# A two-block transformer kernel on one core: convolution taps spread anew, GpSimd taken out of the gates, and the end of each residual projection rearranged

## What is computed

```python
def first_block(x, mem, ...):
    mem_n = rmsnorm(mem, norm_mem_w)
    h = x
    h = h + head_group_mixer(rmsnorm(h, norm_mix_w), ...)     # conv_module and retention, then @ w_out
    h = h + memory_cross_attention(rmsnorm(h, norm_xattn_w), mem_n, xq_w, xkv_w, xo_w)
    h = h + sq_relu_mlp(rmsnorm(h, norm_mlp_w), mlp_up_w, mlp_down_w)
    return rmsnorm(h, norm_f_w)

def conv_module(a, b, conv_w, conv_b, ln_w, ln_b):
    u = a * sigmoid(b)
    y = depthwise causal convolution of u, 31 taps, 512 channels
    return silu(layer norm of y)

def second_block(x, mem, ...):
    x = x + hybrid_mixer(rms_norm(x, norm_mix_g), ...)        # ends in merged @ w_out
    x = x + memory_cross_attention_2(rms_norm(x, norm_xa_g), mem, ...)
    x = x + swiglu(rms_norm(x, norm_ffn_g), w_gate, w_up, w_down)
    return rms_norm(x, final_g)
```

## Time and profile before

| | |
|---|---|
| three runs | 981.06, 982.01, 983.94 us; median 982.01 |
| profiled execution | 980.71 us, of which the span of the program's instructions is 979.0 |
| PE busy | 930.6 us of the span (95%) |
| DVE, ACT, POOL busy | 651.3, 475.1, 12.6 us |
| granted TensorE clock, mean | 0.987 |

### The profile page before, as it was taken

The page is one execution under the profiler, slowest core; times in us unless marked ns, Lnnn a source line. Parts: engine busy times, 40 slices in busy tenths (PEclk is TensorE's granted clock), DMA queues, the critical chain, the costliest instruction groups (busy, mean ns, idle before and its releaser), DMA issues.

```text
span 979.0 us, 15122 instructions
## 1 busy us (share of the span) xinstructions
PE 930.6 (95%) x6344; PEld 858.0 (88%) x6344; DVE 651.3 (67%) x933; ACT 475.1 (49%) x533; POOL 12.6 (1%) x40
## 2 busy tenths in 40 slices
PE   6899999599989999999999999999899899999996
PEld 6788998479879999999899999999798799999995
DVE  5799879959665555555865886765776555555555
ACT  6666435256454444444545636653474453343342
POOL 1100000000000000000000000000000000000000
PEclk9989999799999999999999999999999999999998
DMA  9646535325335565565555535545443346556551
GB/s 323 227 154 229 169 130 175 126 93 168 127 129 173 181 201 175 185 200 173 178 189 172 173 130 172 167 152 194 150 155 115 129 148 204 179 177 199 182 172 43
DMA packets 112469, 164.47 MB, mean 168 GB/s; under 512 B 2784, under 2 KB 90464, under 8 KB 112416
## 3 DMA queue, kind: packets, MB, share of 16 engines
q1 hardware_dynamic: 111856, 161.87, 49.9%
q0 software_dynamic: 560, 1.84, 0.5%
HBM read 162.64 MB, written 1.05 MB: 167 GB/s over the span
## 4 chain that ended last, share of the span: by engine, by line
PE 83%; DVE 8%; ACT 3%; DMA 3%; issue 2%; SPq 0%; DVEq 0%; ACTq 0%
PE ps L534 27%; PE ps L535 26%; PE ps L536 26%; DVE w_lo L1431 2%; DMA w_ring<-in_w_in 2%; ACT w_hi L1017 1%; DVE xl L1457 1%; ACT xh L1047 1%; PE ps L625 1%; DMA w_ring<-in_w_q_xa 1%; PE ps L661 0%; PE ps L796 0%; DVE h L1487 0%; DVE acc L1960 0%; DVE mem_l L1446 0%
## 5 line engine op out<-in xcount | busy, mean ns | idle before, releaser
L1431 DVE TENSOR_TENSOR w_lo<-w_ring,w_hi 128x2048 fp32r<-128x2048 f32 x147 | 335.7, 2291 | 151.8 <-ACT w_hi L1017 150.4
L534 PE MATMUL ps<-xh,w_hi 128*128 128x256 f32 x1216 | 347.3, 286 | 10.2 <-DVE w_lo L1526 8.9
L535 PE MATMUL ps<-xl,w_hi 128*128 128x256 f32 x1216 | 345.1, 284 | 0.0
L536 PE MATMUL ps<-xh,w_lo 128*128 128x256 f32 x1216 | 345.0, 284 | 0.0
L1017 ACT ACTIVATE w_hi<-w_ring 128x2048 fp32r<-128x2048 f32 x147 | 279.6, 1909 | 101.6 <-DMA w_ring<-in_w_in 28.5
L534 PEld LDWEIGHTS ps<-xh,w_hi 128*128 128x128 f32 x1216 | 234.1, 193 | 13.3 <-DVE w_lo L1526 8.9
L535 PEld LDWEIGHTS ps<-xl,w_hi 128*128 128x128 f32 x1216 | 234.3, 193 | 0.7
L536 PEld LDWEIGHTS ps<-xh,w_lo 128*128 128x128 f32 x1216 | 234.3, 193 | 0.0
L534 PE MATMUL ps<-w_hi,xh 128*128 128x512 f32 x192 | 77.7, 405 | 7.7 <-DVE w_lo L1431 5.1
L534 PE MATMUL ps<-w_hi,ff_h 128*128 128x512 f32 x216 | 84.3, 390 | 0.0
L535 PE MATMUL ps<-w_lo,ff_h 128*128 128x512 f32 x216 | 84.2, 390 | 0.0
(11 more groups left out here) (289 smaller groups left out, 1129.4 us busy)
## 6 DMA issues: line engine op xcount, KB each, us to landing
w_ring<-in_w_in SPq DMA_DIRECT2D x36, 1024.0 KB, 5.1
w_ring<-in_mlp_up_w SPq DMA_DIRECT2D x16, 1024.0 KB, 5.5
w_ring<-in_mlp_down_w SPq DMA_DIRECT2D x16, 1024.0 KB, 4.8
w_ring<-in_w_gate_ffn SPq DMA_DIRECT2D x11, 1024.0 KB, 5.3
w_ring<-in_w_up_ffn SPq DMA_DIRECT2D x11, 1024.0 KB, 5.3
w_ring<-in_w_down_ffn SPq DMA_DIRECT2D x11, 1024.0 KB, 5.0
w_ring<-in_xkv_w SPq DMA_DIRECT2D x8, 1024.0 KB, 5.7
w_ring<-in_w_out SPq DMA_DIRECT2D x8, 1024.0 KB, 4.9
```

The lines of the kernel that those rows point to most:

```text
L534: pe.matmul(o, lh, rh, start=first, stop=False)
L535: pe.matmul(o, lh, rl, start=False, stop=False)
L536: return pe.matmul(o, ll, rh, start=False, stop=last)
L1431: dve.tensor_tensor(w_lo[:, s, :], w_ring[:, s, :], w_hi[:, s, :].bitcast(F32), ALU.subtract).then_inc(lo_done, 1)
```

## The change

1. **Gates.** `scale_sigmoid` on GpSimd is gone. DVE multiplies `a` with the scales into `u_pad` and later `u_pad` with the sigmoid; `sig1` has two buffers, both gates' first halves come early.
2. **Memory transposes** stand between slabs 6 and 7 on PE. ACT splits slab 8 before the memory, DVE too.
3. **Taps** are spread anew over the same places; the last ones now stand behind `lo(26)`.
4. **Around the convolution's norm** PE does the variance before the tb 1 half of slab 27, and slab 28 in one piece.
5. **Boundaries.** The last slab is done for tb 1 by column halves (`form_b_last`), the first of which signals `half_done`; DVE's `lo(nxt + 1)` stands behind the splits, not ahead of the residual's addition.
6. **Attention output.** The last `hi` and `lo` of the output projection stand ahead of the split of the last head.
7. **The end.** Column halves there too; addition and gain alternate; GpSimd has no part; the square root takes six operations, not nine, and one operation ahead of it is gone.

```diff
+            def form_b_last(i, k0, xt, kks, half, last, step=0):
+                pe.wait_ge(lo_done, weight_count(i) + step)
+                wh, wl = slab(i, D)
+                c = slice(half * HALF, (half + 1) * HALF)
+                for kk in kks:
+                    mm = mm3(tok(2 + half), (xt[0][:, k0 + kk, P:S], xt[1][:, k0 + kk, P:S]), (wh[:, kk, c], wl[:, kk, c]),
+                             False, last and kk == kks[-1])
+                return mm
...
-                for j in (2, 3):
-                    form_b_rows(i0 + j, 2 * order[j], xt, (1,), False, j == 3).then_inc(slab_used, 1)
-                    if j == 2:
-                        between()
+                form_b_rows(i0 + 2, 2 * order[2], xt, (1,), False, False).then_inc(slab_used, 1)
+                between()
+                form_b_last(i0 + 3, 2 * order[3], xt, (0, 1), 0, True).then_inc(half_done, 1)
+                form_b_last(i0 + 3, 2 * order[3], xt, (0, 1), 1, True).then_inc(slab_used, 1)
...
             form_b_half(I_QK, 0, x_t)
-            pe.wait_ge(u_ready, 2)
-            memory_transpose(N_MEM, mem_tok)
-            form_b_half(I_RV, 2, x_t)
+            def first_memory():
+                pe.wait_ge(u_ready, 2)
+                memory_transpose(N_MEM, mem_tok)
+            form_b_half(I_RV, 2, x_t, first_memory)
...
                 out_hi(2)
+                hi(i_o + 3)
                 out_hi(3)
-                hi(i_o + 3)
...
                 lo(nxt)
-                if n != R_XA:
-                    lo(nxt + 1)
                 for tb in range(TB):
                     update_block(tb)
                     raw_split_lo(n, tb)
-                if n == R_XA:
-                    lo(nxt + 1)
+                lo(nxt + 1)
                 lo(nxt + 2)
...
-                dve.tensor_tensor(sig1[:, :, :], blocks(feat(2 * j + 1)), row_of_scales(0), ALU.mult).then_inc(sig_in, 1)
+                dve.tensor_tensor(sig1[j][:, :, :], blocks(feat(2 * j + 1)), row_of_scales(0), ALU.mult).then_inc(sig_in, 1)
+                dve.wait_ge(tables_ready, 2 + ROPE_HALF)
+                dve.tensor_tensor(u_pad[:, 2 * j:2 * j + 2, CONV_W - 1:], blocks(feat(2 * j)), row_of_scales(0), ALU.mult).then_inc(u_scaled, 1)
...
-                conv(5)
+                conv((9, 10, 10, 8)[j])
...
             lo(22)
+            conv(2)
...
             lo(24)
-            conv(6)
+            conv(10)
...
             lo(25)
-            conv(8)
+            conv(9)
             lo(26)
-            conv(9)
+            conv(len(order))
             lo(27)
-            conv(9)
             lo(28)
-            conv(len(order))
             value_rests(1, v2_lo)
...
+            def column_rsqrt(v, y, t):
+                after(dve.tensor_scalar(y.bitcast(I32), v.bitcast(I32), -0.5, RSQRT_MAGIC, ALU.mult, ALU.add))
+                for three in (3.0, 12.0, 768.0):
+                    after(dve.tensor_scalar(t, v, y, y, ALU.mult, ALU.mult))
+                    after(dve.scalar_tensor_tensor(y, t, -three, y, ALU.add, ALU.mult))
```

More of the change, by code:

```diff
@@ L223, in build @@
         m1 = cursor[0]
-        sig1 = at("sig1", [P, 2, S], m1)
+        sig1 = [at(f"sig1_{j}", [P, 2, S], m1 + 2 * S * j) for j in range(2)]
         rope_t = at("rope_t", [P, 4, 256], m1)
@@ L601, in form_b_half @@
                     mm.then_inc(slab_used, 1)
+                    if between and j == 0:
+                        between()
             def memory_transpose(n, src):
@@ L816, in _ @@
             pe.wait_ge(conv_lo, 2)
-            for j in (2, 3):
-                form_b_rows(I_OUT1 + j, 2 * OUT1_ORDER[j], x_t, (1,), False, j == 3).then_inc(slab_used, 1)
-                if j == 2:
-                    raw_transpose(R_XA, 0, UPD[I_OUT1])
+            form_b_rows(I_OUT1 + 2, 2 * OUT1_ORDER[2], x_t, (1,), False, False).then_inc(slab_used, 1)
+            raw_transpose(R_XA, 0, UPD[I_OUT1])
+            form_b_last(I_OUT1 + 3, 2 * OUT1_ORDER[3], x_t, (0, 1), 0, True).then_inc(half_done, 1)
+            form_b_last(I_OUT1 + 3, 2 * OUT1_ORDER[3], x_t, (0, 1), 1, True).then_inc(slab_used, 1)
             raw_transpose(R_XA, 1, UPD[I_OUT1])
@@ L842, in mlp1 @@
                     mm.then_inc(tb0_done, 1)
-                    for c in range(2):
-                        form_b_rows(i + 2 + c, 2 * c, u_t, (1,), False, c == 1, step=step).then_inc(slab_used, 1)
-                        if c == 0:
-                            raw_transpose(R_MIX2, 0, UPD[I_FF1])
+                    form_b_rows(i + 2, 0, u_t, (1,), False, False, step=step).then_inc(slab_used, 1)
+                    raw_transpose(R_MIX2, 0, UPD[I_FF1])
+                    form_b_last(i + 3, 2, u_t, (0, 1), 0, True, step=step).then_inc(half_done, 1)
+                    form_b_last(i + 3, 2, u_t, (0, 1), 1, True, step=step).then_inc(slab_used, 1)
                 else:
@@ L994, in _ @@
             glu_in(ff2_gate(G2 - 1), gate_done=G2 - 1, up_done=G2 - 1)
-            for tb in range(TB):
-                pe.wait_ge(glu_lo, G2 - 1)
-                mm = form_b_rows(N_SLABS - 2, 0, (ff_h, ff_l), (tb,), False, False)
-                if tb == 1:
-                    mm.then_inc(slab_used, 1)
-                pe.wait_ge(glu_lo, G2)
-                form_b_rows(N_SLABS - 1, 2, (ff_h, ff_l), (tb,), False, True).then_inc(tb0_done if tb == 0 else slab_used, 1)
+            pe.wait_ge(glu_lo, G2 - 1)
+            form_b_rows(N_SLABS - 2, 0, (ff_h, ff_l), (0,), False, False)
+            pe.wait_ge(glu_lo, G2)
+            form_b_rows(N_SLABS - 1, 2, (ff_h, ff_l), (0,), False, True).then_inc(tb0_done, 1)
+            form_b_last(N_SLABS - 2, 0, (ff_h, ff_l), (0, 1), 0, False)
+            form_b_last(N_SLABS - 1, 2, (ff_h, ff_l), (0, 1), 0, True).then_inc(half_done, 1)
+            form_b_last(N_SLABS - 2, 0, (ff_h, ff_l), (0, 1), 1, False).then_inc(slab_used, 1)
+            form_b_last(N_SLABS - 1, 2, (ff_h, ff_l), (0, 1), 1, True).then_inc(slab_used, 1)
         @block.scalar
@@ L1478, in add @@
                         dve.wait_ge(tb0_done, upd + 1)
+                    elif 2 * part < parts:
+                        dve.wait_ge(half_done, upd + 1)
                     else:
@@ L2060, in _, with gained @@
             dve.wait_ge(gain_loaded, 16 * (G_FINAL + 1))
-            for tb in range(TB):
-                for half in range(2):
-                    add(tb, half, 2)
-                for half in range(2 - tb):
-                    c = slice(half * HALF, (half + 1) * HALF)
-                    dve.wait_ge(h_updated, 6 * UPD[I_FF2] + 2 * tb + half + 1)
-                    after(dve.tensor_tensor(xn[:, tb, c], h[:, tb, c], gain[:, c], ALU.mult))
+            def column_rsqrt(v, y, t):
[3 more added lines that the diff above has]
+                    after(dve.scalar_tensor_tensor(y, t, -three, y, ALU.add, ALU.mult))
+            def gained(tb, half):
+                c = slice(half * HALF, (half + 1) * HALF)
+                dve.wait_ge(h_updated, 6 * UPD[I_FF2] + 2 * tb + half + 1)
+                dve.scalar_tensor_tensor(xn[:, tb, c], h[:, tb, c], -1.0 / 256, gain[:, c], ALU.mult, ALU.mult).then_inc(last_gain, 1)
+            for tb in range(TB):
+                add(tb, 0, 2)
+                if tb == 1:
+                    gained(tb, 0)
+                add(tb, 1, 2)
+                if tb == 0:
+                    gained(tb, 0)
+                gained(tb, 1)
                 dve.wait_ge(last_sq, 2 * tb + 2)
                 v, y, t = nv[:, tb:tb + 1], ny[:, tb:tb + 1], nt[:, tb:tb + 1]
-                after(dve.tensor_tensor(v, sq_last[:, 2 * tb:2 * tb + 1], sq_last[:, 2 * tb + 1:2 * tb + 2], ALU.add))
-                after(dve.tensor_scalar(v, v, 1.0 / D, EPS, ALU.mult, ALU.add))
-                rsqrt(v, y, t)
+                after(dve.scalar_tensor_tensor(v, sq_last[:, 2 * tb:2 * tb + 1], D * EPS, sq_last[:, 2 * tb + 1:2 * tb + 2], ALU.add, ALU.add))
+                column_rsqrt(v, y, t)
                 dve.sem_inc(y_ready, 1)
+                dve.wait_ge(last_gain, 2 * tb + 2)
                 dve.tensor_scalar(xn[:, tb, 0:HALF], xn[:, tb, 0:HALF], y, None, ALU.mult).then_inc(out_lead, 1)
```

61 lines of the change are left out of this document (25 added, 36 removed).

## The result

The changed kernel takes 958.58 us (median of four runs, 958.35 to 958.92), the kernel before 982.98 us beside it (981.06 to 985.69). The ratio is 0.975, 95% interval 0.9725 to 0.9775. The forecast was 962.0 us, its range 957.5 to 968.5: the time lies inside it, near the fast end. The profiled execution took 958.75 us with a span of 956.8, where 960.8 was forecast.

The account below looks back on a forecast made before the run. PE, busy 930.6 of 979.0 us, bounds the kernel, so only its losses can go; 1.3 − 0.7 − 0.8 + 9.7 + 8.8 + 1.6 = 19.9 off the median 982.0 gives 962.0 us, range 957.5 to 968.5.

Parts of the forecast that it names:

- A: Opening up to slab 8: gain 1.3 us from less DVE work and idle time, less 0.7 for a low clock.
- B: Slabs 8 to 26: 25 taps moved forward fit into DVE's spare 12.85 us; loss 0.8 us.
- rival 1: Moved taps become PE's wait, at lo 25 and 26; costs 4 to 8 us, 966 to 970; chance 0.20.
- clock term of A: Slab 8 may begin at half speed behind PE's new wait: between nothing and 1.8 us, taken as 0.7.
- rival 3: A moved tap costs its whole 0.48 us, not 0.40: +2.0 us, 964; chance 0.07.
- C: End of the values to slab 29: 29.32 us becomes 19.6, 15.5 of work plus three waits; gain 9.7 us.
- D: Boundaries R_MLP, R_MIX2, R_XA2, R_FF2: waits for w_lo and h go; column halves cost nothing; gain 8.8 us.
- 0.6 given back behind R_MLP: Behind R_MLP the split of the first MLP activations comes 1.1 us late, of which 0.6 is taken for PE.
- rival 2: Column halves do work at the five boundaries and the end: 4.9 us, so 957; chance 0.10.
- E: Kernel's end: shorter small chain 0.8, no GpSimd product beside it 0.7, better packing 0.1; gain 1.6 us.
- the shorter chain: At the end, the small chain falls from twelve operations to eight, 0.20 us apart: gain 0.8 us.
- rivals 4 and 5: 4: TensorE stays at half clock behind slab 8's wait, 985 or 987; 5: taps still end last, 980; chance 0.02 each.

Follow-up runs that it names:

- n_early: Changed kernel with four taps ahead of the last key split, lo 29 behind the root, six taps moved from ahead of slab 8 to behind it: 953.83 us.
- u_taps: Changed kernel with the late part of the convolution's taps put back as in the kernel before: 967.80 us, ratio 0.9843.
- b_taps: Kernel before with only the late part of the convolution's taps as in the changed kernel: 975.04 us, ratio 0.9919.
- u_halves: Changed kernel with the last slabs in one piece again, half_done waited for nowhere: 959.73 us, ratio 0.9762.
- n_banks: Changed kernel, column halves kept, with the first block's transposes at each boundary in four PSUM banks, not two: 955.37 us, ratio 0.9721.
- n_banks_whole: Changed kernel with the first block's transposes at each boundary in four PSUM banks and the last slabs in one piece: 959.02 us, ratio 0.9757.

## Why the prediction came out right, step by step

**A, the opening.** Right in the start of slab 8, and the mechanism fits the traces. DVE sets the pace: in n_early six taps fewer on it brought slab 8 forward. The two groups that had run beside GpSimd's products now take 0.16 and 0.73 us, as taken. In the stretch of the earlier trace rows DVE is busy 1.2 us less (29.90 for 31.08) and idle 0.8 us less (1.3 for 2.1), where the sum had 0.8 and 0.5. Slab 8 starts 1.4 us sooner relative to the first matmul (forecast 1.3) and PE waits 4.4 us (forecast 4 to 5). The term that was mis-sized is the clock's: 0.7 in the sum, 1.7 in the profiled execution (3.41 us at half clock), up to 2.9 in the traces of the other kernels (5.9 us in u_taps). I had put it at the lower half of its range for the reason that the rotary transposes break the wait, and they stand ahead of it, not in it (58.92 to 59.99).

**B, slabs 8 to 26.** The taps fitted in, as forecast, and rival 1 (waits for `lo` 25 and 26) fell: no such wait is in the trace. The 0.8 us charged for the two taps ahead of the retention's norm did not come (0.34 us of wait there, 0.35 before). The errors in the clock term of A and in this 0.8 cancelled, which was luck: a loss of 1.5 forecast for the two, 1.4 measured. Moved taps cost 0.40 us each (the eleven behind `lo` 26 take 4.4, from 173.24 to 177.68), so rival 3 fell too.

**C, slabs 27 and 28.** 19.6 forecast, 19.1 measured, with waits of 1.6 and 1.8 (forecast 1.6 and 2.1) and some 0.2 for the squares (0.4). u_taps and b_taps show that the taps made it. What I did not see is that part 4 of the change may add nothing to it: b_taps has 19.3 without, with a wait ahead of slab 27 that is 0.8 longer.

**D, the boundaries.** 8.8 forecast, 10.2 measured from slab 29 on. The waits went as forecast; two things were mis-sized. The first is the 0.6 given back behind R_MLP. The split of the first MLP activations did come late, by 0.9 us against R_MLP's transposes (1.1 taken), but PE waits only 0.27 for it; that wait lies in the row of R_MIX2 in the table. The second is what a removed wait is worth, which I took as the wait's own length. In the traces matmuls of 512 columns start 0.23 us apart and last 0.39 (their ends are modelled), so a wait read from end to start leaves out 0.16. And the first work behind a wait is slower: the eight transposes of R_MIX2 and R_XA2 took 1.31 and 1.25 us behind their waits, and take 1.03 without. These two make up most of the 0.2 to 0.3 us that R_MLP, R_XA2 and R_FF2 gave above the forecast, and the 0.15 of slab 29, which started behind a wait of 1.4 us before and does so no more. That the halves are hidden was right, and is shown by three kernels (u_halves, n_banks, n_banks_whole); rival 2, which gave them 4.9 us, fell.

**E, the end.** 1.6 forecast, 1.2 measured. The mis-sized term is the shorter chain: I priced all its operations at 0.20 us from start to start, but the three with two column operands take 0.31. Without GpSimd's 0.7 the twelve took 2.26 us and the eight take 1.86, so that 0.4 was saved, not 0.8. The 0.7 of GpSimd's product was right.

**The sum.** 19.9 forecast, 22.2 in the traces: 1.4 more in D, 0.6 at the first matmul that is no effect, 0.5 in C, 0.1 each in A and B, and −0.4 in E. The medians moved by 24.4. That the timed runs of before spent more time at half clock than its profiled one is likely, as others of its runs had mean clocks of 0.983 to 0.989 and the profiled one 0.987, but it is not shown for these four. Neither of rivals 4 and 5 came.
